# A decoder layer with attention, RWKV-7 and 32 experts: the second norm applied behind the router and row transposes, both moved into the output projection; selection on whole tiles; outputs in pairs

## The chip, the cores and the metric

One core of one Trainium2 chip. The metric is the device time of one execution in microseconds.

## What is computed

One layer for 256 prompt tokens and 8 sample tokens (T = 264), D = 1024, all float32. Attention and RWKV-7 mixing give `m`; then

```
x  = x + gate1(c) * (m @ w_o)
h2 = rms_norm(x, norm2) * (1 + scale2(c)) + shift2(c)
logits = h2 @ w_router + b_router              # 32 experts
top 4 per token, gates = softmax of those 4
y  = sum over chosen experts of gate * (swiglu(h2 @ w1[e] + b1[e]) @ w2[e] + b2[e])
x  = x + gate2(c) * y
```

`c` is one vector for the prompt and one for each sample. Caches and states are outputs too.

## The kernel before

Everything is kept with features on the 128 partitions: `XT` and `HT` are `[128, 8 chunks, 264 tokens]`. Each engine has its own hand-written program in `build`, joined by semaphores; a `group()` on TensorE and its twin on ScalarE hand out four PSUM banks in turn, in the order of `a_order`. `chain(...)` makes VectorE wait for its own last instruction. SyncE (SP) streams all weights in chunks of 2 MB into ring slots 0 to 5 and later two slots (6, 7) in `arena`, each issued when the slot's last user is done.

Ahead of the experts TensorE runs, in line order: modulation 10 and its transpose, modulation 11 (L1174 to 1176, the modulation matmuls at L812, 32 columns each, four beside each other), group-norm sums (L1179), mixers `pa` and `pb` (L1190), the output projection (L1203: eight steps of eight matmuls, banks 4 to 7), eight sums of squares (L1207). VectorE adds the residual (L1655 to 1658); ScalarE squares (L688). Then VectorE computes the norm for each token (L1363 to 1365) and `h2` in two halves (L1374 to 1378), TensorE the router product (L1214), 24 transposes of `h2` to token rows (L1222) which ScalarE copies into `XR` (L698), and transposes of the logits (L1227).

Selection (L1679 to 1738, VectorE) takes the best 8 of 32 per token for three token tiles (128, 128, 8), builds a 0/1 mask `MSK` with one comparison and three accumulating ones per tile (L1685, L1687); TensorE turns the mask into each token's position in its expert by triangular products (L1234, L1238); VectorE makes ranks `POSM` (L1704, L1710) and 64 slots per expert (L1721). A round serves 64 tokens of every expert; here there is one round.

Expert i on TensorE: four chunks of `w1` (L1296), combine of expert i-1 (L1269) which VectorE adds to `YA` (L1749), transposes (L1304), gather of the next expert's rows through `OH` (L1245, copy L714 or L727, transposes L1251, copy L716 or L733), two chunks of `w2` (L1323). Line 369 loads the last two chunks of expert 0 when the projection is done; lines 376 onward load each next chunk when its slot is used. At the end: combine, eight updates of `XT` (L1778), 24 transposes (L1338), six copies on ScalarE (L741), three stores (L393).

```
for c in (4, 2):
    sp.wait_ge(*chunk_used(max(i for i in range(len(stream)) if slots_of[i] == c)))
    sp.dma_start(slot_tile(c, c), expert_chunk(0, c)).then_inc(sem[f"ring{c}"], 16)
```

## Time and profile before

| | us |
|---|---|
| median of 3 runs | 1339.03 (1333.54 to 1339.52) |
| profiled execution | 1338.93 |
| its span | 1337.1 |
| TensorE busy | 1259.7 (94%) |
| VectorE, ScalarE busy | 452.7, 300.6 |
| DMA | 467.03 MB, 349 GB/s mean |

The span runs from the first to the last recorded instruction. Matmul busy time overlaps (matmuls are pipelined), so it doesn't say how near TensorE is to its limit. A float32 matmul is recorded as two instructions, a transpose as one.

### The profile page before, as it was taken

To read this page: it belongs to the slowest core of one execution; us is meant where nothing else is said; L and a number is where in the kernel's file an instruction comes from. 1 tells how busy PE (TensorE), PEld (TensorE's weight loads), DVE (VectorE), ACT (ScalarE), POOL (GpSimd) and SP (SyncE) were. 2 spreads that over 40 slices of the span, in tenths; PEclk is the share of its full clock that TensorE was granted. 3 is DMA by queue.
4 is the path that set the end of the run, shared out by engine and by line. 5 is a ranking of instruction groups with operands and counts; after the bars stand their busy time and mean duration, and the time that the engine had idled before them with its cause. 6 is when DMAs were issued, how large, how long until landed. Compare 5 with 4: busy or idle time off the path is not lost.

```text
span 1337.1 us, 21010 instructions
## 1 busy us (share of the span) xinstructions
PE 1259.7 (94%) x8316; PEld 633.5 (47%) x8316; DVE 452.7 (34%) x1062; ACT 300.6 (22%) x553; POOL 53.8 (4%) x67
## 2 busy tenths in 40 slices
PE   6998997989969999999999999999999999999997
PEld 4787776977833334333333333333333333333333
DVE  2145658335262223322233222233222223322223
ACT  3012441211022112222122121222121122212112
POOL 0000530300000000000000000000000000000000
PEclk9899998999979999999999999999999999999999
DMA  9966351139437999999999999999999999999993
GB/s 368 344 233 246 111 162 59 40 132 376 194 126 308 425 429 428 428 430 428 428 428 429 428 429 428 429 429 428 429 428 428 429 428 428 428 430 427 429 428 134
DMA packets 55606, 467.03 MB, mean 349 GB/s; under 512 B 5141, under 2 KB 7449, under 8 KB 29690
## 3 DMA queue, kind: packets, MB, share of 16 engines
q1 hardware_dynamic: 53354, 461.05, 83.0%
q0 software_dynamic: 1664, 5.20, 1.4%
q8 instruction: 35, 0.57, 0.2%
q10 hardware_dynamic: 544, 0.13, 0.0%
q14 instruction: 9, 0.07, 0.0%
HBM read 463.89 MB, written 5.09 MB: 351 GB/s over the span
## 4 chain that ended last, share of the span: by engine, by line
PE 72%; DMA 20%; DVE 4%; ACT 2%; issue 1%; SPq 0%; DVEq 0%
PE ps L1296 24%; DMA ring<-in_w 18%; PE ps L1323 13%; PE ps L1245 5%; PE ps L843 5%; PE ps L1269 4%; PE ps L833 3%; PE ps L1203 2%; PE ps L1304 2%; DMA ring<-in_w_mod 2%; PE ps L1190 1%; PE ps L1251 1%; PE ps L852 1%; ACT PT L727 1%; PE ps L812 1%
## 5 line engine op out<-in xcount | busy, mean ns | idle before, releaser
L1296 PE MATMUL ps<-ring,PT 128*64 128x512 f32 x1536 | 337.5, 593 | 10.7 <-DMA ring<-in_w 9.9
L1749 DVE TENSOR_TENSOR SQ<-ps,SQ 128x528 f32<-128x528 f32 x132 | 84.1, 699 | 617.9 <-PE ps L1269 617.9
L1296 PEld LDWEIGHTS ps<-ring,PT 128*64 128x64 f32 x1536 | 109.6, 137 | 232.7 <-issue 209.0
L1323 PE MATMUL ps<-ring,PT 128*64 128x512 f32 x768 | 170.1, 596 | 0.0
L722 ACT COPY HT<-ps 128x512 f32<-128x512 f32 x64 | 34.4, 589 | 396.9 <-PE ps L1296 396.9
L1296 PE MATMUL ps<-arena,PT 128*64 128x512 f32 x512 | 113.5, 593 | 3.9 <-DMA arena<-in_w 3.9
L1323 PEld LDWEIGHTS ps<-ring,PT 128*64 128x64 f32 x768 | 53.2, 137 | 99.8 <-issue 99.8
L1245 PE MATMUL ps<-XR,PT 128*64 128x512 f32 x396 | 93.9, 610 | 1.6 <-DVE PT L1721 1.6
L1269 PE MATMUL ps<-PT 64*128 64x264 f32 x528 | 76.3, 408 | 0.8 <-ACT PT L735 0.8
L1296 PEld LDWEIGHTS ps<-arena,PT 128*64 128x64 f32 x512 | 36.5, 137 | 78.2 <-issue 69.1
L843 PE MATMUL ps<-HT,ring 128*128 128x264 f32 x304 | 70.7, 394 | 0.0
L1269 PEld LDWEIGHTS ps<-PT 64*128 64x128 f32 x528 | 45.3, 185 | 44.9 <-issue 27.6
L735 ACT COPY PT<-ps 128x512 f32<-128x512 f32 x32 | 18.8, 586 | 206.1 <-PE ps L1323 206.1
L843 PEld LDWEIGHTS ps<-HT,ring 128*128 128x128 f32 x304 | 58.6, 194 | 10.8 <-issue 0.8
L833 PE MATMUL ps<-HT,ring 128*128 128x264 f32 x208 | 54.3, 414 | 4.9 <-DMA ring<-in_w_in 3.5
L1323 PE MATMUL ps<-arena,PT 128*64 128x512 f32 x256 | 56.7, 596 | 0.0
L1245 PEld LDWEIGHTS ps<-XR,PT 128*64 128x64 f32 x396 | 25.9, 138 | 46.0 <-issue 46.0
L833 PEld LDWEIGHTS ps<-HT,ring 128*128 128x128 f32 x208 | 40.5, 202 | 14.2 <-DMA ring<-in_w_in 3.8
L722 ACT ACT_TABLE_LOAD x32 | 41.1, 1283 | 0.9 <-issue 0.4
L725 ACT ACT_TABLE_LOAD x32 | 41.1, 1283 | 0.6
L1727 DVE TENSOR_SCALAR PT<-cst,PT 128x128 f32<-128x128 f32 (+1 forms) x96 | 27.1, 339 | 28.4 <-DVE PT L1770 25.8
L1304 PE MATMUL ps<-cst,HT 128*128 128x128 f32 x256 | 35.0, 280 | 0.0
(383 smaller groups left out, 1153.9 us busy)
## 6 DMA issues: line engine op xcount, KB each, us to landing
ring<-in_w SPq DMA_DIRECT2D x144, 2048.0 KB, 28.9
arena<-in_w SPq DMA_DIRECT2D x48, 2048.0 KB, 28.8
ring<-in_w_mod SPq DMA_DIRECT2D x12, 2048.0 KB, 12.7
ring<-in_w_in SPq DMA_DIRECT2D x9, 2048.0 KB, 14.9
ring<-in_w_o SPq DMA_DIRECT2D x2, 2048.0 KB, 16.6
ring<-in_w_pa SPq DMA_DIRECT2D x1, 2048.0 KB, 12.8
ring<-in_w_pb SPq DMA_DIRECT2D x1, 2048.0 KB, 9.2
bias_rows<-bias_by_distance POOLq DMA_DIRECT2D x1, 1536.0 KB, 14.0
```

Of the source, the lines that this page charges most:

```text
L722: act.copy(UR[:, h, :].rearrange("p (f r) -> p f r", f=4), ps[:, 2 + h, :].rearrange("p (r f) -> p f r", f=4)).then_inc(sem["ur_evac"], 1)
L725: act.activation(US_, UG, ACT.Sigmoid, scale=1.702).then_inc(sem["us_ready"], 1)
L833: last = mm(ps[:, GATE_BANK[b], 0:T], w[:, k, s * P:s * P + P], HT[:, k, :], start=(k == 0), stop=(k == KD - 1))
L843: last = mm(bank[:, 0:T], w[:, k, s * P:s * P + P], HT[:, k, :], start=(k == 0), stop=(k == KD - 1))
L1203: last = mm(ps[:, 4 + k % 4, 0:T], w[:, i, (k % 4) * P:(k % 4) * P + P], HT[:, i, :], start=(i == 0), stop=(i == KD - 1))
L1245: last = mm(ps[64 * s:64 * s + 64, 0, :], OH[:, n, :], XR[:, n, s * 512:s * 512 + 512], start=(n == 0), stop=(n == 2))
L1269: last = mm(ps[:, bank + s, 0:T], YS[64 * s:64 * s + 64, p * P:p * P + P], GT[64 * s:64 * s + 64, :], start=True, stop=True)
L1296: last = mm(ps[64 * lin:64 * lin + 64, 2 + hh, :], XG[:, k % 4, k // 4, :], slot_tile(slot, c)[:, k % 2, lin * FE + hh * 512:lin * FE + hh ...
L1304: last = tr(ps[:, 2 + hh, f * P:f * P + P], UR[:, hh, f * P:f * P + P], ID)
L1323: last = mm(ps[64 * hh:64 * hh + 64, 4, :], AC[:, f, :], slot_tile(slot, c)[:, f % 4, hh * 512:hh * 512 + 512], start=(f == 0), stop=(f == ...
L1727: v.tensor_scalar(OG[0:nt, n, :], IO2[0:nt, :], POSM[0:nt, n, col], GATE[0:nt, n, col], ALU.is_equal, ALU.mult)
L1749: v.tensor_tensor(YA[:, p::4, :], ps[:, bank:bank + 2, 0:T], YA[:, p::4, :], ALU.add).then_inc(sem["comb_used"], 1)
```

## The change

- The norm is no longer applied before router and transposes. ScalarE and VectorE form `Z = x * norm2 * (1 + scale2)`; router and row transposes work on `Z`, and the per-token factor `1/rms` is applied to the logits and, by ScalarE's scaled copies, to the rows of the two prompt tiles. The shift's part of the logits is computed ahead (`CX`, `CL`), the shift's part of the rows is row 8 of the third tile in `XR` (samples hold their difference to it), which every slot gathers.
- Row transposes of step k-1 and half of the router product stand inside the projection, which uses two banks in place of four. Router matmuls go to four column groups and are summed in a product with `K_S4`. Squares are summed on VectorE into `ACC`, and across partitions with one column.
- Selection runs on whole tiles: one comparison and one reduction for the mask, positions in six products, first gather ahead of gates, ranks of later rounds and `GTE`.
- The slots of the two large tiles are compared in one instruction in every expert; the third tile has nine rows.
- At the end the sum so far is applied before the last combine, whose four pairs go straight to `XT`; copies of the outputs are shared by ScalarE and VectorE.
- The clearing of `YA` on GpSimd waits for the first gather; the router bias is loaded as one row; `MR` moves to `RS`. On VectorE, behind the key norm (L1448), the bias of modulation columns 24 to 32 is added and the sample differences `DSX` are formed.

New and kept lines of the diff (removed lines and unnamed edits are left out; the kernel before stands above):

```diff
+c[:, K_S4:K_S4 + NE] = p % NE == np.arange(NE)
...
+Z, SQ1, MSK4 = SQ, view(PT, 2582, 2, T), view(PT, 3110, 3, 4, NE)
+CX, CL = RS[:, P:P + 136], view(PT, 2318, 2, NE)
+DSX, brr, x1s = view(SSf, 0, KD, 9), SSf[0:1, 72:72 + NE], SSf[:, 104:112]
...
+    pool.wait_ge(sem["h2r_done"], 3)
+    pool.wait_ge(sem["xg_evac"], 1)
     pool.memset(YA[:, :, :], 0.0).then_inc(sem["comb_used"], 1)
...
+    bank = group()
+    act.copy(CX[:, 0:P], bank[:, 0:1].broadcast_to([P, P]))
+    act.copy(CX[:, P:P + NS], bank[:, 1:9]).then_inc(sem["a_evac"], 1)
+    act.wait_ge(sem["st_kv"], 64)
+    for s in range(2):
+        bank = group_bank()
+        act.copy(pairs_apart(XR[0:9, 2, s * 512:s * 512 + 512]), pairs_read(bank[0:9, :])).then_inc(sem["a_evac"], 1)
     mod_rows(11)
...
+    bank = group()
+    act.copy(CL[:, 0, :], bank[:, 0:NE])
+    act.copy(CL[0:NS, 1, :], bank[0:NS, NE:2 * NE]).then_inc(sem["a_evac"], 1)
     for k in range(KD):
+        act.wait_ge(sem["x1_ready"], 2 * k + 1)
+        act.mul(Z[:, k, 0:NP], XT[:, k, 0:NP], A1[:, k, 0:1]).then_inc(sem["zp_ready"], 1)
         act.wait_ge(sem["x1_ready"], 2 * k + 2)
...
+        if k >= 3:
+            act.wait_ge(sem["acc_done"], k - 2)
+        act.activation(SQ1[:, k % 2, :] if k else ACC, XT[:, k, :], ACT.Square).then_inc(sem["sq2_ready"], 1)
     act.wait_ge(sem["ms_ready"], 2)
...
+    act.activation(st[:, 70:73], st[:, 70:73], ACT.Sqrt).then_inc(sem["sqrt_done"], 1)
+    act.wait_ge(sem["rs_ready"], 1)
+    act.wait_ge(sem["st_s"], 32)
+    for n in range(2):
+        act.wait_ge(sem["h2r_done"], n + 1)
+        for s in range(2):
+            act.mul(pairs_apart(XR[:, n, s * 512:s * 512 + 512]), pairs_read(ps[:, 2 * n + s, :]),
+                    st[:, 70 + n:71 + n]).then_inc(sem["h2r_evac"], 1)
+    act.wait_ge(sem["top_ready"], 1)
+    act.activation(RNK[:, :, :], LG[:, :, :], ACT.Exp).then_inc(sem["top_exp"], 1)
...
+    pe.wait_ge(sem["ld_r"], 32)
+    bank = group()
+    for k in range(KD):
+        g = k % 4
+        mm(bank[32 * g:32 * g + NE, 0:9], wr[:, k, :], modT[:, 24 + k, :], start=(k < 4), stop=(k >= 5))
+    mm(bank[0:NE, 0:9], brr, ONE[0:1, 0:9], start=False, stop=True).then_inc(sem["a_done"], 1)
+    for s in range(2):
+        bank = group()
+        for k in range(4):
+            last = tr(bank[0:9, k * P:k * P + P], DSX[:, 4 * s + k, :], ID)
+        last.then_inc(sem["a_done"], 1)
     modulation(11)
...
+    bank = group()
+    pe.wait_ge(sem["a_evac"], a_end("cl"))
+    mm(bank[:, 0:NE], CX[:, 0:P], cst[:, K_S4:K_S4 + NE], start=True, stop=True)
+    mm(bank[0:NS, NE:2 * NE], CX[:, P:P + NS], cst[:, K_S4:K_S4 + NE], start=True, stop=True).then_inc(sem["a_done"], 1)
+    def rows(k, tiles):
+        for n in tiles:
+            t0, nt = TILES[n]
+            bank = 2 * n + k // 4 if n < 2 else 6 - k // 4
+            last = tr(ps[0:nt, bank, (k % 4) * P:(k % 4) * P + P], Z[:, k, t0:t0 + nt], ID)
+        return last
+    def logits(ks):
+        for k in ks:
+            last = mm(ps[32 * (k % 4):32 * (k % 4) + NE, 7, 0:T], wr[:, k, :], Z[:, k, :], start=(k < 4), stop=(k >= 4))
+        return last
     for k in range(KD):
         w = weights("wo", k // 4)
...
+        if k >= 2:
+            pe.wait_ge(sem["x1_ready"], 2 * k - 2)
         for i in range(KD):
...
+            last = mm(ps[:, 4 + k % 2, 0:T], w[:, i, (k % 4) * P:(k % 4) * P + P], HT[:, i, :], start=(i == 0), stop=(i == KD - 1))
         last.then_inc(sem["wo_done"], 1)
...
+        if k == 1:
+            pe.wait_ge(sem["a_evac"], a_end("cm"))
+        if k:
+            pe.wait_ge(sem["zp_ready"], k)
+            pe.wait_ge(sem["zs_ready"], k)
+            rows(k - 1, range(3 if k <= 4 else 2))
+        if k == 4:
+            logits(range(4))
+    pe.wait_ge(sem["zp_ready"], KD)
+    pe.wait_ge(sem["zs_ready"], KD)
+    logits(range(4, KD)).then_inc(sem["lg_done"], 1)
+    pe.wait_ge(sem["acc_done"], KD - 2)
+    pe.wait_ge(sem["sq2_ready"], KD)
+    for n, (t0, nt) in enumerate(TILES):
+        mm(ps[0:nt, 4, 96 + n:97 + n], ACC[:, t0:t0 + nt], ONE[:, 0:1], start=True, stop=False)
+        last = mm(ps[0:nt, 4, 96 + n:97 + n], SQ1[:, 1, t0:t0 + nt], ONE[:, 0:1], start=False, stop=True)
     last.then_inc(sem["ss_done"], 1)
...
+    pe.wait_ge(sem["lgt_ready"], 1)
+    for n, (t0, nt) in enumerate(TILES):
+        last = mm(ps[0:nt, 7, 320 + n * NE:320 + n * NE + NE], LGT[:, t0:t0 + nt], cst[:, K_S4:K_S4 + NE], start=True, stop=True)
+    last.then_inc(sem["lg_done"], 1)
+    for n in range(2):
+        rows(KD - 1, [n]).then_inc(sem["h2r_done"], 1)
+    for k in range(4, KD):
+        last = rows(k, [2])
+    last.then_inc(sem["h2r_done"], 1)
     pe.wait_ge(sem["msk_ready"], 1)
...
+    mm(ps[:, 4, 160:256], ONE, MSK[:, 0:1, :].broadcast_to([P, 3, NE]), start=True, stop=False)
+    mm(ps[:, 4, 160:192], cst[:, K_US:K_US + P], MSK[:, 1, :], start=False, stop=False)
+    mm(ps[:, 4, 192:256], ONE, MSK[:, 1:2, :].broadcast_to([P, 2, NE]), start=False, stop=False)
+    mm(ps[:, 4, 192:224], cst[0:NS, K_US:K_US + P], MSK[0:NS, 2, :], start=False, stop=False)
+    mm(ps[:, 4, 224:256], ONE[0:NS, :], MSK[0:NS, 2, :], start=False, stop=True)
+    mm(ps[:, 4, 128:160], cst[:, K_US:K_US + P], MSK[:, 0, :], start=True, stop=True).then_inc(sem["pos_done"], 1)
...
+        for n, rows_in in enumerate((P, P, NS + 1)):
             for s in range(2):
...
+                last = mm(ps[64 * s:64 * s + 64, 0, :], OH[0:rows_in, n, :], XR[0:rows_in, n, s * 512:s * 512 + 512],
+                          start=(n == 0), stop=(n == 2))
         last.then_inc(sem["xr_done"], 1)
...
+    pe.wait_ge(sem["h2r_evac"], 4)
+    pe.wait_ge(sem["h2s_ready"], 1)
     pe.wait_ge(sem["oh_ready"], 1)
     gather()
+    pe.wait_ge(sem["xr_evac"], 1)
+    gather_transposed()
     pe.wait_ge(sem["gte_ready"], 1)
     scatter_transposed(GTE)
...
     pe.wait_ge(sem["rounds_ready"], 1)
...
+    pe.wait_ge(sem["ys_evac"], rounds * NE + 1)
+    pe.wait_ge(sem["gt_evac"], rounds * NE + 1)
+    pe.wait_ge(sem["comb_used"], rounds * (NE * 4) + 1)
+    def outputs(p, tiles):
+        for n in tiles:
+            t0, nt = TILES[n]
+            for s in range(2):
+                last = tr(ps[0:nt, 2 * n + s if n < 2 else 6 + s, p * P:p * P + P], XT[:, 4 * s + p, t0:t0 + nt], ID)
+        return last
+    for p in range(4):
+        if p >= 2:
+            pe.wait_ge(sem["x2_ready"], p - 1)
+        for s in range(2):
+            last = mm(ps[:, 4 + 2 * (1 - p % 2) + s, 0:T], YS[64 * s:64 * s + 64, p * P:p * P + P], GT[64 * s:64 * s + 64, :],
+                      start=True, stop=True)
+        last.then_inc(sem["comb_done"], 1)
+        if p >= 2:
+            outputs(p - 2, range(2))
+    pe.wait_ge(sem["x2_ready"], 3)
+    outputs(2, range(2))
+    for p in range(3):
+        outputs(p, [2])
+    pe.wait_ge(sem["x2_ready"], 4)
+    outputs(3, [0]).then_inc(sem["fin_done"], 1)
+    outputs(3, [1]).then_inc(sem["fin_done"], 1)
+    outputs(3, [2]).then_inc(sem["fin_done"], 1)
...
     dve.wait_ge(sem["a_evac"], a_end("modT11"))
...
+    for lo, hi in ((16, 24), (32, 48)):
+        out, bias = add_bias(lo, hi)
+        chain(v.tensor_tensor(out, out, bias, ALU.add))
     chain(v.tensor_scalar(modT[:, 16:24, :], modT[:, 16:24, :], 0.5, None, ALU.mult))
+    chain(v.scalar_tensor_tensor(out=A1[:, :, :], in0=modT[:, 32:40, :], scalar=1.0,
+                                 in1=PC[:, PCOL["norm2"]:PCOL["norm2"] + KD].unsqueeze(2).broadcast_to([P, KD, 9]),
+                                 op0=ALU.add, op1=ALU.mult))
+    v.memset(st[:, 70:73], 1.0)
+    v.memset(LG, 0.0)
+    v.memset(POSM, 0.0)
+    chain(v.memset(GTE, 0.0))
     for k in range(KD):
         dve.wait_ge(sem["wo_done"], k + 1)
...
+        src = ps[:, 4 + k % 2, :]
+        chain(v.tensor_tensor(x1s, src[:, NP:T], modT[:, 16 + k, 1:9], ALU.mult))
         v.scalar_tensor_tensor(out=XT[:, k, 0:NP], in0=src[:, 0:NP], scalar=modT[:, 16 + k, 0:1],
                                in1=XT[:, k, 0:NP], op0=ALU.mult, op1=ALU.add).then_inc(sem["x1_ready"], 1)
...
+        done(v.tensor_tensor(XT[:, k, NP:T], XT[:, k, NP:T], x1s, ALU.add), "x1_ready", 2 * k + 2)
+        v.tensor_tensor(Z[:, k, NP:T], XT[:, k, NP:T], A1[:, k, 1:9], ALU.mult).then_inc(sem["zs_ready"], 1)
+        if 1 <= k < KD - 1:
+            dve.wait_ge(sem["sq2_ready"], k + 1)
+            done(v.tensor_tensor(ACC, ACC, SQ1[:, k % 2, :], ALU.add), "acc_done", k)
     IE = cst[:, K_IE:K_IE + NE]
...
     dve.wait_ge(sem["lg_done"], 1)
...
+    v.tensor_copy(LGT, ps[:, 7, 0:T]).then_inc(sem["lgt_ready"], 1)
+    dve.wait_ge(sem["ss_done"], 2)
+    v.tensor_scalar(st[:, 70:72], ps[:, 4, 96:98], 1.0 / D, 1e-5, ALU.mult, ALU.add)
+    v.tensor_scalar(st[0:NS, 72:73], ps[0:NS, 4, 98:99], 1.0 / D, 1e-5, ALU.mult, ALU.add).then_inc(sem["ms_ready"], 1)
+    dve.wait_ge(sem["sqrt_done"], 2)
+    done(v.reciprocal(st[:, 70:73], st[:, 70:73]), "rs_ready", 1)
+    dve.wait_ge(sem["a_evac"], a_end("cm"))
     dve.wait_ge(sem["lg_done"], 2)
...
+    tiles(lambda n, nt: v.scalar_tensor_tensor(out=LG[0:nt, n, :], in0=ps[0:nt, 7, 320 + n * NE:320 + n * NE + NE], scalar=st[0:nt, 70 + n:71 + n],
+                                               in1=CL[0:nt, n // 2, :], op0=ALU.mult, op1=ALU.add))
+    tiles(lambda n, nt: v.max(mx8[:, n, :], LG[:, n, :]))
+    tiles(lambda n, nt: v.max_index(ix8[:, n, :], mx8[:, n, :], LG[:, n, :]))
+    chain(v.tensor_copy(ixf[:, :, :], ix8[:, :, :]))
+    chain(v.tensor_tensor(MSK4, IE.unsqueeze(1).unsqueeze(1).broadcast_to([P, 3, 4, NE]),
+                          ixf[:, :, 0:4].unsqueeze(3).broadcast_to([P, 3, 4, NE]), ALU.is_equal))
+    done(v.tensor_reduce(MSK[:, :, :], MSK4.rearrange("p n j e -> p n e j"), AX.X, ALU.add), "msk_ready", 1)
+    v.tensor_tensor(LG[:, :, :], LG[:, :, :], mx8[:, :, 0:1].broadcast_to([P, 3, NE]), ALU.subtract).then_inc(sem["top_ready"], 1)
+    dve.wait_ge(sem["h2r_done"], 3)
+    for s in range(2):
+        for b in range(2):
+            lo = b * 2 * P
+            rows_of_x = XR[0:NS, 2, s * 512 + lo:s * 512 + lo + 2 * P].rearrange("t (j p) -> t j p", j=2)
+            last = v.scalar_tensor_tensor(out=rows_of_x, in0=ps[0:NS, 6 - s, lo:lo + 2 * P].rearrange("t (p j) -> t j p", j=2),
+                                          scalar=st[0:NS, 72:73], in1=rows_of_x, op0=ALU.mult, op1=ALU.add)
+    last.then_inc(sem["h2s_ready"], 1)
     dve.wait_ge(sem["pos_done"], 1)
...
+    tiles(lambda n, nt: v.scalar_tensor_tensor(out=POSM[0:nt, n, 0:NE], in0=ps[0:nt, 4, 128 + n * NE:160 + n * NE], scalar=1.0,
+                                               in1=MSK[0:nt, n, :], op0=ALU.add, op1=ALU.mult))
...
     def gather_slots(col):
...
+        v.tensor_tensor(OH[:, 0:2, :], IO.unsqueeze(1).broadcast_to([P, 2, C]), POSM[:, 0:2, col].broadcast_to([P, 2, C]), ALU.is_equal)
+        return v.tensor_scalar(OH[0:NS + 1, 2, :], IO[0:NS + 1, :], cst[0:NS + 1, K_BB:K_BB + 1], POSM[0:NS + 1, 2, col],
+                               ALU.mult, ALU.is_equal)
...
     gather_slots(slice(0, 1)).then_inc(sem["oh_ready"], 1)
...
+    chain(v.tensor_reduce(st[:, 80:81], ps[:, 4, 224:256], AX.X, ALU.max))
...
+    dve.wait_ge(sem["top_exp"], 1)
+    chain(v.tensor_tensor(RNK[:, :, :], RNK[:, :, :], MSK[:, :, :], ALU.mult))
+    chain(v.tensor_reduce(st[:, 73:76], RNK[:, :, :], AX.X, ALU.add))
+    chain(v.reciprocal(st[:, 73:76], st[:, 73:76]))
+    chain(v.tensor_tensor(RNK[:, :, :], RNK[:, :, :], st[:, 73:76].unsqueeze(2).broadcast_to([P, 3, NE]), ALU.mult))
+    done(v.tensor_copy(GTE.rearrange("p n (s e) -> p n s e", s=2)[:, :, :, 0:NE], RNK[:, :, :].unsqueeze(2).broadcast_to([P, 3, 2, NE])), "gte_ready", 1)
+    chain(v.tensor_copy(GATE[:, :, 0:MAXR * NE].rearrange("p n (r e) -> p n r e", e=NE),
+                        RNK[:, :, :].unsqueeze(2).broadcast_to([P, 3, MAXR, NE])))
+    for q in range(1, MAXR):
+        tiles(lambda n, nt: v.tensor_scalar(POSM[0:nt, n, q * NE:q * NE + NE], POSM[0:nt, n, 0:NE], -1.0 * q * C, None, ALU.add))
...
+    dve.wait_ge(sem["comb_used"], rounds * (NE * 4) + 1)
     chain.base, chain.count = rounds * (NE * LINKS) + links_before, 0
     chain(v.tensor_tensor(YA[:, :, NP:T], YA[:, :, NP:T], modT[:, 40:48, 1:9], ALU.mult))
...
+    v.tensor_tensor(XT[:, :, NP:T], XT[:, :, NP:T], YA[:, :, NP:T], ALU.add)
     for k in range(KD):
         last = v.scalar_tensor_tensor(out=XT[:, k, 0:NP], in0=YA[:, k, 0:NP], scalar=modT[:, 40 + k, 0:1],
                                       in1=XT[:, k, 0:NP], op0=ALU.mult, op1=ALU.add)
+    chain(last)
+    for p in range(4):
+        bank = 4 + 2 * (1 - p % 2)
+        dve.wait_ge(sem["comb_done"], rounds * (NE * 4) + p + 1)
+        chain(v.tensor_tensor(YA[:, p::4, NP:T], ps[:, bank:bank + 2, NP:T], modT[:, 40 + p:48:4, 1:9], ALU.mult))
+        v.tensor_tensor(XT[:, p::4, NP:T], XT[:, p::4, NP:T], YA[:, p::4, NP:T], ALU.add)
+        for s in range(2):
+            k = 4 * s + p
+            last = v.scalar_tensor_tensor(out=XT[:, k, 0:NP], in0=ps[:, bank + s, 0:NP], scalar=modT[:, 40 + k, 0:1],
+                                          in1=XT[:, k, 0:NP], op0=ALU.mult, op1=ALU.add)
         last.then_inc(sem["x2_ready"], 1)
+    for n, (_, nt) in enumerate(TILES):
+        dve.wait_ge(sem["fin_done"], n + 1)
+        v.tensor_copy(fin[0:nt, n, 512:D], ps[0:nt, 2 * n + 1 if n < 2 else 7, :]).then_inc(sem["fin_half"], 1)
```

## Rows read from the trace of the kernel before

**Rows 1.** Windows: us busy (instructions) per engine, granted clock, DMA share, GB/s

```profile
395.00:400.00 5.00, 3.92 (x12) 1.26 (x12) 3.20 (x25) 0.00 (x0) 0.00 (x0) 0.55 0.00 0
...
405.00:410.00 5.00, 5.00 (x26) 1.72 (x24) 0.00 (x0) 0.00 (x0) 0.00 (x0) 1.00 0.41 108
...
600.00:900.00 300.00, 297.59 (x1486) 112.71 (x1484) 84.81 (x226) 68.79 (x105) 0.00 (x0) 1.00 1.01 429
```

**Rows 2.** Chain of waits, expert loop: start us, us, what

```profile
403.43 13.95 PE ps L1296 x64
...
488.12 13.73 PE ps L1296 x64
...
516.27 13.73 PE ps L1296 x64
...
1245.01 3.65 PE ps L1296 x16
...
1303.74 3.65 PE ps L1296 x16
```

**Rows 3.** Line 369, the two loads behind the output projection

```profile
DMA to landing us min/median/max: 7.6/9.8/12.1
```

**Rows 4.** Timeline ahead of the projection: start us, us, engine, operation, [idle before <-releaser]

```profile
126.33 1.04 PE L892 MATMUL ps<-cst,PT 128*9 128x128 f32 x8
...
286.67 0.47 PE L1168 MATMUL ps<-cst,arena 128*128 128x32 f32 x2 [2.54 <-issue]
...
303.86 1.95 PE L812 MATMUL ps<-ring,cT 128*32 128x128 f32 x64
...
309.16 6.75 DVE L1631 RECIPROCAL SQ<-SQ 128x1056 f32<-128x1056 f32 x1 [11.93 <-ACT SQ L683]
...
320.46 3.83 PE L1190 MATMUL ps<-PT,ring 128*128 128x264 f32 x16 [0.20 <-DVE HT L1627]
```

**Rows 5.** Chain of waits, output projection to gather

```profile
339.53 28.75 PE ps L1203 x128
...
368.28 3.57 PE ps L1207 x16
...
392.89 1.57 PE ps L1238 x6
...
396.07 4.46 PE ps L1245 x12
```

**Rows 6.** Timeline, projection to first expert, and a gather in the loop

```profile
386.41 1.09 PE L1222 MATMUL ps<-cst,HT 128*128 128x128 f32 x8
...
389.01 1.76 DVE L1687 SCALAR_TENSOR_TENSOR arena<-cst,ixf,arena 128x32 f32<-128x32 f32 x9
...
401.37 0.59 ACT L714 COPY PT<-ps 128x512 f32<-128x512 f32 x1
...
420.58 2.80 PE L1245 MATMUL ps<-XR,PT 128*64 128x512 f32 x12
```

**Rows 7.** Groups of instructions, 339 to 404 us: busy us, mean ns of one

```profile
L1656 DVE SCALAR_TENSOR_TENSOR XT<-ps,modT,XT 128x256 f32<-128x256 f32 x8 | 3.9, 484 | 0.3
...
L688 ACT ACTIVATE SQ<-XT 128x264 f32<-128x264 f32 x8 | 3.4, 423 | 57.1 <-DVE XT L1658 57.1
...
L1374 DVE TENSOR_TENSOR HT<-XT,RS 128x1056 f32<-128x1056 f32 x2 | 2.5, 1254 | 0.0
...
L1655 DVE TENSOR_TENSOR A<-ps,modT 128x8 f32<-128x8 f32 x8 | 1.3, 167 | 23.0 <-PE ps L1203 23.0
```

**Rows 8.** Windows with short pauses of TensorE, columns as in rows 1

```profile
226.00:230.00 4.00, 3.17 (x42) 2.06 (x36) 3.80 (x4) 0.39 (x1) 1.27 (x1) 1.00 0.34 79
...
285.00:288.00 3.00, 1.33 (x5) 1.16 (x6) 1.65 (x5) 0.00 (x0) 0.00 (x0) 0.80 0.78 232
```

**Rows 9.** Timeline of the tail

```profile
1322.58 2.31 PE L1269 MATMUL ps<-PT 64*128 64x264 f32 x16 [0.76 <-ACT PT L735]
...
1333.27 0.72 SPq L393 DMA_DIRECT2D out_y_sample<-ring  x1
```

204 lines of the change are left out of this document (40 added, 164 removed).

## The prediction

> **What bounds the kernel now.** I read the busy shares by window first, then the chain of waits in order of time, then the timelines of three places. In the long middle both TensorE and the DMA engines look full [rows 1]. The chain tells them apart. In the first half of the expert loop one expert follows the next on TensorE every 516.27 - 488.12 = 28.15 us. Late in the loop the chain runs through weight loads, and two experts take 1303.74 - 1245.01 = 58.73 us, so 29.37 us each [rows 2]. A chunk of 2 MB (2.097 million bytes) at 429 GB/s takes 4.9 us [rows 1], six of them 29.3; the loop begins limited by TensorE, with eight chunks in hand, loses 1.2 us of that lead on each expert, and ends limited by the DMA stream. So a faster or slower expert body would change nothing as long as it stays under 29.4 us.
>
> What matters is when the stream restarts. In the window from 395 to 400 us the DMA share is 0.00: every slot is full, and the next chunk waits for expert 0 to use its first one. It restarts between 405 and 410 us (share 0.41), some 3.7 us after the first expert matmul at 403.43 [rows 1, 2], and is full from there on. About 182 chunks of 4.9 us follow before the last one on which the chain waits. A microsecond by which the first expert starts earlier is therefore a microsecond off the end, as long as it does not start before expert 0's last two chunks have landed, up to 12.1 us after the output projection [rows 3]. The other place that counts is the tail behind the last load.
>
> The change adds work on TensorE ahead of the output projection, lengthens the projection, and shortens what lies between it and the first expert.
>
> **Ahead of the projection.** Between the transpose of modulation 10 and modulation 11 TensorE gets nine small packed matmuls (18 instructions) and eight transposes of nine columns. The packed modulation runs 64 instructions in 1.95 us, so 18 take 0.55; eight such transposes took 1.04 [rows 4]. That is 1.6 us. Behind it come modulation 11, the group-norm sums, the square root and the 6.75 us reciprocal on VectorE, which the last mixer chunks wait for (TensorE stands 0.20 us until a VectorE result at 320.46) [rows 4]. So I count all 1.6 on the path; the bounds are 0, if the delay is absorbed, and 2.5, if ScalarE's four new copies stand in front of its row copy. The two VectorE subtractions far ahead, behind the key norm, cost nothing: VectorE then waits for the decay, and no queue is behind them. The wait of ScalarE for the k and v stores costs nothing either; they were issued over 100 us before. The constant's last product is four instructions straight in front of the projection; two with 128-column weights took 0.47 [rows 4], so 0.7, between 0.4 and 0.9. The new preamble on VectorE (bias in two parts, A1, four memsets) is about 2.1 us and hides behind the first 3.6 us of the projection; without that cover it would be paid in full.
>
> **In the projection.** It takes 28.75 us for 128 instructions, 0.225 each [rows 5]. Eighteen transposes go between its steps, one pair of them behind its last. Eight back to back took 1.09 [rows 6], so 0.136 each: 2.2 us ahead of the end. Four router matmuls go in beside each other on four column groups: as two instructions of 264 columns 0.45, as eight 1.8; packed, like the modulation, I take 0.45. With two banks in place of four, step k waits for the evacuation of k-2, a whole step of 3.6 us old, and the transposes for a copy that is ready about 1.25 us after its step (VectorE 0.17 and 0.48, ScalarE 0.42) [rows 7]. VectorE's work per step grows to some 1.9 us. No new wait bites. The projection ends at 368.28 + 1.6 + 0.7 + 2.2 + 0.45 = 373.2.
>
> **From there to the first expert.** Before: 403.43 - 368.28 = 35.15 us. It held eight sums of squares (3.57) [rows 5], the norm and modulation on VectorE, router product, 24 transposes, and a selection in small steps. Now, in order:
> - last residual and scaled copy 1.25, second half of the router product 0.45
> - sums of squares: eight wide instructions by 0.223 and four narrow by 0.1, 2.2
> - mean, square root and reciprocal of three columns 1.05; beside them the transposing product of the logits
> - scaling, max and index at the spacing of the old small steps, 1.3; cast 0.2; one comparison of 384 elements and one reduction. A 256-element operation took 0.484 and a 1056-element one 1.254 [rows 7], so 0.6 each. In all 2.7
> - positions: twelve instructions with 128-column weights. Six took 1.57 [rows 5]: 3.1. The four row fix-ups of the sample tile (about 2.0 on VectorE) lie beside them; if positions took less than 2, they would be late next
> - ranks 0.4, slots 0.5, handing over 0.1: 1.0
> - gather 4.0. It took 4.46 here and 2.80 inside the loop [rows 5, 6]; I take nearly the first, because the granted clock was 0.55 from 395 to 400 [rows 1], mostly the lower level of 1.2 GHz, and TensorE will again stand some 2 us before the positions. After a pause of 2.54 us up to 286.67 the granted clock was 0.80 in the window around its end [rows 4, 8]
> - copy, four transposes, copy: 403.43 - 401.37 [rows 2, 6], and 0.15: 2.2. The gate's copy no longer stands in front.
>
> The sum is 17.95 us. The first expert then starts at 391.2, 12.2 earlier. The gates, further ranks and the round count run on VectorE until about then, and the loop's first need of them is 14 us later. The zeroing of YA moves from under the old norm to under the first expert, 1.9 us on GpSimd with 12 in hand.
>
> A rule speaks against the size of one term. The nine accumulations of the old mask took 1.76 us, 0.195 each for 32 elements [rows 6]; with the three comparisons before them they are 2.3, and two operations of 0.6 give back 1.1. The Trainium skill (VectorE: DVE Perf Modes, the errata section) has 58 cycles at 0.96 GHz plus one per element for an operation in SBUF; by it the twelve would be 1.1 us, the two 0.9, and merging would give back 0.2. This trace doesn't agree with its price of a small operation; by its price of the two large ones the end would come 0.3 sooner, at 1323.8. I go by the rows.
>
> **Inside an expert.** Three comparisons become two and the last gather tile has nine rows; TensorE streams the same columns. Under the DMA limit this is worth nothing.
>
> **The tail.** Before, the last combine starts at 1322.58; four additions, two small steps and eight updates follow, TensorE transposes behind them, and the last of six copies lets the third store go at 1333.27, 3.8 us before the end [rows 9]. Now all but the last expert is added in while the last products run. Each of four pairs takes 0.17 + 0.16 + two of 0.48 overlapping, 1.25, from 1323.1: the last at 1328.2. Two transposes for each large tile, one pair of copies on two engines each 0.6, the last store at 1330.7: 2.6 us sooner, between 1.5 and 3.5.
>
> **The sum** is made against the profiled execution, 1338.93 us (span 1337.1 and 1.8 around it), 0.1 under the median of 1339.03: 1338.93 - 12.2 - 2.6 = 1324.1.
>
> **Rivals.**
> A. Clock kept and the insertion hidden: new TensorE pauses are 1 to 2 us, and from 226 to 230, with TensorE busy 3.17 of 4 us in short bursts, it stayed at 2.4 GHz [rows 8]. Then positions 0.5, the gather 1.2 and upstream up to 1.6 less: 1320.8. Against it, the window after 284 [rows 8]. Chance 0.20.
> B. Dearer chain: VectorE's broadcast comparison and transposed reduction, which the trace doesn't show, at twice my price (1.2), router matmuls not packed (2.7 for both halves), fix-ups late (1.0), a tail worth only 1.5: 1330.1. Chance 0.10.
> C. The stream doesn't restart with the first expert, and only the tail is gained: 1336.3. For it, the DMA share stays at 1.01 through the loop; against it, the idle 25 us in front [rows 1]. Chance 0.05.
> D. Slower: the per-expert chain passes the DMA period. The slot comparisons for the next expert feed TensorE's gather; the two-input form with broadcasts would have to hold VectorE until TensorE waits in every expert. From 29.4 us on each added microsecond costs 31, so it must add 1.2 before it decides; at 2.0 the end is 0.8 x 31 - 14.8 = 10 us later, 1349. Against it: VectorE is busy 84.81 of 300 us in the loop [rows 1]. Chance 0.03.
> E. It doesn't do what it says, or router values change the number of rounds: no change or far slower. 0.02.
>
> **Numbers.** The forecast itself has 0.60 and runs from 1321.5 to 1327.5. Taking in A and half of B, the range is 1317.5 to 1330.5. A measurement of this kernel can tell about 0.5%, 6.7 us, from no change; below 1332.3 is faster. That is the forecast, A and B: 0.90. Within 0.5% are C and half of E: 0.06. Slower are D and the other half: 0.04.
>
> **What would show it.** The first expert matmul near 391; the projection's end near 373, modulation 11 1.6 later; selection ready about 7.7 after the projection; DMA restarting at about 395; the same 29.4 us between late experts; the last store issued 2.6 sooner after the last combine. It is wrong if the projection shows gaps of its own, if ScalarE is the releaser ahead of modulation 11 or the square root, or if experts take over 29.4.

## The result, and the profile after

The changed kernel takes 1322.76 us (median, 1321.98 to 1327.27) against 1339.15 of the kernel before: ratio 0.9894, 95% interval 0.986 to 0.9928. The forecast was 1324.1. It was right in sign and size, but what follows from modulation 10 on became only 11.7 to 12.3 us shorter, where 14.8 were forecast; the rest of the 16 us lies ahead of modulation 10, where no gain was forecast. Single executions of the kernel before at 1483 to 1485 us, with a granted clock of 0.84, are left out of every comparison.

The page of the changed kernel begins so (busy us, share of the span, instructions):

```profile
span 1321.2 us, 21010 instructions
PE 1259.3 (95%) x8339; PEld 626.5 (47%) x8339; DVE 453.8 (34%) x1034; ACT 300.1 (23%) x554; POOL 52.9 (4%) x66
```

The chain of waits of the changed kernel, from modulation 10 to the last expert (start us, us, what):

```profile
297.06 1.93 PE ps L834 x64
301.09 1.93 PE ps L834 x64
306.32 6.76 DVE SQ L1687
...
871.18 13.73 PE ps L1347 x64
...
899.48 6.89 PE ps L1347 x32
906.53 31.58 DMA ring<-in_w
...
1231.94 3.65 PE ps L1347 x16
...
1290.68 3.65 PE ps L1347 x16
```

The last chunk is waited for at 1290.68 instead of 1303.74 [rows 2], 13.1 sooner. The reader can also see where the loop changes hands: until 906 one expert follows the next on TensorE, behind that the chain runs through the loads, 1290.68 - 1231.94 = 58.74 for two experts, as before [rows 2].

The stretch between the output projection and the first expert, in the timeline of the changed kernel (start us, us, engine, line, operation, idle before and its releaser):

```profile
369.87 0.66 PE L1246 MATMUL ps<-SQ,arena 128*32 128x264 f32 x8 [1.17 <-ACT SQ L715]
370.46 0.38 PE L1270 MATMUL ps<-cst,arena 128*128 128x1 f32 x2
...
371.72 0.16 DVE L1732 TENSOR_SCALAR st<-ps 128x2 f32<-128x2 f32 x1 [0.69 <-PE ps L1271]
...
372.54 0.56 DVE L1745 SCALAR_TENSOR_TENSOR arena<-ps,st,PT 128x32 f32<-128x32 f32 x3 [0.15 <-PE ps L1275]
...
374.38 0.56 DVE L1750 TENSOR_TENSOR PT<-cst,ixf 128x384 f32<-128x384 f32 x1
374.97 0.80 DVE L1752 TENSOR_REDUCE arena<-PT 128x96 f32<-128x384 f32 x1
...
375.83 0.74 PE L1284 MATMUL ps<-arena,cst 128*128 128x96 f32 x2 [2.62 <-DVE arena L1752]
...
378.96 0.37 DVE L1764 SCALAR_TENSOR_TENSOR PT<-ps,arena 128x32 f32<-128x32 f32 x3 [1.33 <-PE ps L1289]
...
380.02 5.58 PE L1295 MATMUL ps<-XR,PT 128*64 128x512 f32 x12 [1.10 <-DVE PT L1772]
...
388.16 15.62 PE L1347 MATMUL ps<-ring,PT 128*64 128x512 f32 x64
```

The last line is from the timeline of TensorE alone. The projection's last step ends at 368.50, so this chain is 19.66 us long; before it was 35.15. And its tail, behind the last product:

```profile
1309.67 1.16 PE L1397 MATMUL ps<-PT 64*128 64x264 f32 x8 [0.76 <-ACT PT L759]
...
1317.55 0.50 SPq L406 DMA_DIRECT2D out_y_sample<-ring  x1
```

From the last combine to the end of the span: 1321.2 - 1309.67 = 11.53, before 1337.1 - 1322.58 = 14.52 [rows 9].

Where the 15.49 us between projection and first expert were won can be read off the two timelines, with two lines of the kernel before:

```profile
386.52 0.37 DVE L1679 COPY arena<-ps 128x32 f32<-128x32 f32 x3 [0.43 <-PE ps L1227]
...
388.45 0.52 DVE L1685 TENSOR_SCALAR arena<-cst,ixf 128x32 f32<-128x32 f32 x3
```

From the projection's end to VectorE's first reading of the logits for the selection (386.52 before, 372.54 now) it is 18.24 and 4.04 us: 14.2 of the 15.49, against 4.4 us more work ahead of that point. The selection up to the positions took 4.37 (386.52 to 390.89) and takes 3.29, positions to gather 5.18 and 4.19, and the gather with what follows it 7.36 and 8.14, which is 0.8 dearer.

**The head.** Not all of the gain lies where the change is. In the chains of waits modulation 10 starts at 301.27 before and at 297.06 after, and ahead of it the two kernels do the same work but for a few small steps of VectorE (a bias, a subtraction, a copy). PE timelines of the early part, first the kernel before, then the changed one:

```profile
28.77 3.64 PE L798 MATMUL ps<-ring,cT 128*32 128x128 f32 x64 [2.79 <-DMA ring<-in_w_mod]
36.02 16.97 PE L852 MATMUL ps<-HT,ring 128*128 128x264 f32 x64 [1.79 <-DVE HT L1399]
```

```profile
28.98 2.59 PE L820 MATMUL ps<-ring,cT 128*32 128x128 f32 x83 [1.45 <-issue]
34.70 14.48 PE L874 MATMUL ps<-HT,ring 128*128 128x264 f32 x64 [1.79 <-DVE HT L1451]
```

From 18 to 36 us the granted clock is 0.76 before and 1.00 after. So I measure everything from the start of modulation 10 to the end of the span: 1035.83 before, 1024.14 after. From there on the change is worth 11.7; some four of the 16 us are ahead of it.

### The profile page after: what moved, and what is told of

It reads as the page before. It is cut to its first block, busy times and chain, and to the rows that moved or that the text cites. A ratio compares the mean times of both kernels' runs of the same rounds, so it can differ in the third digit from the quotient of the medians.

```text
span 1321.2 us, 21010 instructions
## 1 busy us (share of the span) xinstructions
PE 1259.3 (95%) x8339; PEld 626.5 (47%) x8339; DVE 453.8 (34%) x1034; ACT 300.1 (23%) x554; POOL 52.9 (4%) x66
## 4 chain that ended last, share of the span: by engine, by line
PE 73%; DMA 18%; DVE 5%; ACT 2%; issue 1%; SPq 0%; DVEq 0%
PE ps L1347 24%; DMA ring<-in_w 18%; PE ps L1374 13%; PE ps L1295 6%; PE ps L865 5%; PE ps L1320 4%; PE ps L1254 2%; PE ps L855 2%; PE ps L1355 2%; PE ps L1222 1%; PE ps L1302 1%; ACT PT L751 1%; PE ps L874 1%; PE ps L834 1%; PE ps L1118 1%
## 5 line engine op out<-in xcount | busy, mean ns | idle before, releaser
L1295 PE MATMUL ps<-XR,PT 128*64 128x512 f32 (+1 forms) x396 | 99.7, 622 | 1.1 <-DVE PT L1772 1.1
L1295 PEld LDWEIGHTS ps<-XR,PT 128*64 128x64 f32 (+1 forms) x396 | 22.8, 136 | 53.5 <-issue 53.5
```

Source lines behind the costliest of these rows:

```text
L1295: last = mm(ps[64 * s:64 * s + 64, 0, :], OH[0:rows_in, n, :], XR[0:rows_in, n, s * 512:s * 512 + 512], start=(n == 0), stop=(n == 2))
```

## The experiments

**The head again: is it the program or the run?** The changed kernel unchanged, and the kernel before unchanged.

> The changed kernel once more. In the two profiles at hand it is 15.9 us shorter in span, but 3.8 us of that are there before 53 us, where the two programs are the same: the clock rose at about 20 us in the one and at about 14 us in the other, which then lost it in the wait for weights. Theory A (the front is a matter of the clock's phase in an execution, not of the change): times of both kernels fall in two groups 4 to 5 us apart, and group against group the change is worth 11 to 12.5 us, ratio 0.991. Rival B (the change moves the front): all runs of the changed kernel have the short front, and it stays 15 to 16 us faster, ratio 0.988.

Measured 1323.05 (1322.17 to 1323.68), ratio 0.9891, interval 0.9872 to 0.991. Modulation 10 at 297.75, from there 1023.55. The ratio lies between the two theories. (The rise of the clock "at about 14" and "at about 20 us" is read from durations: the same pair of matmuls takes 1.25 us before and 0.71 behind it. The granted clock of these windows reads 1.00 in both profiles.)

> The kernel before, once more, for a second profile of it. From the start of modulation 11's predecessor (modulation 10 on TensorE) to the end of the span the kernel before took 1035.9 us, the changed kernel 1024.1 and 1023.6 in two profiles; ahead of it the same instructions took 301.2 against 297.1 and 297.8. Theory A (that head is a matter of the clock's phase in each execution): here modulation 10 starts anywhere from 296 to 302, and what follows takes 1035.9 again. Rival B (the change shortens the head): it starts at 301 again.

Measured 1335.47 us in one execution. In its PE timeline the fourth modulation chunk is fast, and the first projection is 0.8 us shorter and begins two microseconds sooner:

```profile
28.31 1.96 PE L798 MATMUL ps<-ring,cT 128*32 128x128 f32 x64 [2.31 <-DMA ring<-in_w_mod]
...
34.14 16.19 PE L852 MATMUL ps<-HT,ring 128*128 128x264 f32 x64 [2.52 <-DMA ring<-in_w_in]
```

Modulation 10 starts at 297.85, where the changed kernel has it, and from there it takes 1035.85, as in the first profile of before. So the same program runs with either head. At equal heads the two kernels stand at 1335.47 and 1323.05: 12.4 us, and 12.3 from modulation 10 on.

Two things about the head stay open. The first is where it comes from: the clock of the first 36 us is a part of it only. In the run a_full (below) that clock is 0.76 as in the first profile of before, and modulation 10 still starts at 297.74; in a_loop1 and a_loop3 it is 0.97 and 0.96, and modulation 10 starts at 300.52 and 300.34. A second place is a piece of 16 projection matmuls behind a pause of 2.53 us shortly ahead of modulation 10: it takes 5.16 us in the changed kernel and 6.68 in a_loop3, where the granted clock behind the pause stays at 0.50 for longer. The second is whether the change has a part in how often a kernel gets the short head. All executions of the kernel before, over four sessions, have a median of 1337.5 (37 of them, 1333.4 to 1340.0, 11 below 1335.6); the nine of the changed kernel have 1323.0, and eight of them lie between 1321.9 and 1323.7. That is 14.5 us between medians, two more than at equal heads. Nothing here shows whether this is chance or the change.

**Can the head be held?** The kernel before with idle matmuls in the waits of its first 36 us.

```
                 slot = slots_of[STREAM_AT["modA", q]]
+                filler((0, 1, 1, 6)[q], 7)
...
+            filler(1, 7)
             pe.wait_ge(sem["mod_a_evac"], 1)
...
             last.then_inc(sem["setup_t"], 1)
+            filler(3, 7)
```

> The kernel before, with matmuls on spare PSUM columns put where TensorE waits for the first weights and the first norm (before the third and fourth modulation chunk, before the transposes and before the first projection). Theory A: the granted clock stays at 1.00 from 25 to 45 us, the first projection (line 852) takes 14.4 us instead of 17.0, and the kernel ends about 4 us sooner than the kernel before in its slower group (about 1334 to 1335), with little scatter. Rival B: no change of the end, because the weights of later projections arrive no sooner.

Measured 1337.69 (1333.88 to 1342.79), ratio 1.0003, interval 0.9987 to 1.0018: nothing. Its timeline tells why (lines of this kernel):

```profile
32.72 1.95 PE L804 MATMUL ps<-ring,cT 128*32 128x128 f32 x64
...
37.83 14.48 PE L860 MATMUL ps<-HT,ring 128*128 128x264 f32 x64 [0.49 <-DVE HT L1407]
```

The clock was held, 14.48 instead of 16.97. But the fillers were more than the waits: the fourth modulation chunk came at 32.72 instead of 28.77, and the projection 1.8 later. Behind the projection this profile is 0.7 us ahead of the first one of before and 2.0 behind the second: what the clock gave, the filling took. It then lost another 2.1 us up to modulation 10, which starts at 302.69; with one profile of twelve executions that part isn't explained.

**Chain: what does the clock cost?** In the changed kernel the granted clock falls in the short pauses behind the projection and stays down through dense work, the gather included. Windows of the changed kernel (length, busy us of PE, PEld, DVE, ACT, POOL, granted clock, DMA share, GB/s):

```profile
370.00:375.00 5.00, 3.21 (x32) 2.28 (x28) 3.11 (x19) 2.56 (x6) 0.00 (x0) 0.95 0.87 364
375.00:380.00 5.00, 3.09 (x12) 2.79 (x13) 3.57 (x12) 1.77 (x3) 0.00 (x0) 0.50 0.99 423
380.00:385.00 5.00, 4.98 (x12) 1.13 (x12) 4.00 (x24) 0.00 (x0) 0.00 (x0) 0.50 0.01 3
385.00:390.00 5.00, 4.18 (x15) 1.95 (x15) 1.75 (x2) 2.53 (x4) 1.83 (x1) 0.50 0.00 0
390.00:395.00 5.00, 5.00 (x22) 1.55 (x20) 0.85 (x5) 0.30 (x1) 0.03 (x1) 0.84 0.27 49
```

Eleven idle matmuls of 256 columns were spread there, into columns of banks 4 and 7 that nothing reads any more (VectorE raises `lg_read` when it has read the logits out of bank 7):

```
+            for _ in range(2):
+                mm(ps[:, 4, 256:512], XT[:, 0, 0:P], XT[:, 1, 0:256], start=True, stop=True)
             pe.wait_ge(sem["zp_ready"], KD)
...
+            pe.wait_ge(sem["lg_read"], 1)
+            filler(5)
             pe.wait_ge(sem["msk_ready"], 1)
...
+            filler(2)
             pe.wait_ge(sem["h2r_evac"], 4)
...
             gather()
+            filler(1)
...
             scatter_transposed(GTE)
+            filler(1)
...
+            dve.sem_inc(sem["lg_read"], 1)
```

> The changed kernel with matmuls of 256 columns on spare PSUM columns where TensorE waits: two behind the projection, five before the positions (behind VectorE's reading of the logits), two before the first gather, one behind it, one behind the gate's transposes. Theory A (all from the positions to the first expert's second chunk runs at the lower clock because of the pauses): positions 2.4 instead of 3.1 us, gather 2.9 instead of 5.0 to 5.6, first expert's w1 part 13.95 instead of 15.6; the load stream restarts about 5 us sooner and the end comes 4 to 6 us sooner. Rival C (the gather is slow because of its nine-row tile or late row copies): the same durations, and the fillers cost up to 1 us.

Measured 1319.16 (1317.36 to 1319.66), ratio 0.9866, interval 0.9847 to 0.9884. Its windows and its timeline, first expert included:

```profile
375.00:380.00 5.00, 4.52 (x26) 3.26 (x26) 4.67 (x18) 2.35 (x4) 0.00 (x0) 1.00 0.99 426
380.00:385.00 5.00, 4.94 (x25) 1.97 (x23) 3.54 (x21) 1.45 (x3) 0.53 (x1) 1.00 0.13 56
...
390.00:395.00 5.00, 5.00 (x27) 1.59 (x24) 0.00 (x0) 0.00 (x0) 0.00 (x0) 1.00 0.91 374
```

```profile
376.54 0.46 PE L1293 MATMUL ps<-arena,cst 128*128 128x96 f32 x2 [0.32 <-DVE arena L1765]
...
379.42 2.94 PE L1304 MATMUL ps<-XR,PT 128*64 128x512 f32 x12 [0.15 <-DVE PT L1785]
...
384.63 13.95 PE L1359 MATMUL ps<-ring,PT 128*64 128x512 f32 x64
```

The clock stays at 1.00. The gather takes 2.94 instead of 5.58 (4.96 in the second profile), positions to gather 2.9 instead of 4.2, the first expert's first part 13.95 instead of 15.62, and it starts at 384.63. The load stream restarts at 388.33 instead of 393.53. From modulation 10 to the end 1017.95: 5.6 to 6.2 less than in the two profiles of the changed kernel. That is the price of the lower clock in this stretch, and it reaches the end. Rival C, a gather slowed by its nine-row tile or by late row copies, is out: the same gather runs in 2.94.

**Transposes behind the logits.** All 24 row transposes go behind the router product, so that the projection carries none.

```
-                if k:
+                if k == 4:
                     pe.wait_ge(sem["zp_ready"], k)
                     pe.wait_ge(sem["zs_ready"], k)
-                    rows(k - 1, range(3 if k <= 4 else 2))
...
+            for n in range(3):
+                for k in range(KD):
+                    last = rows(k, [n])
+                last.then_inc(sem["h2r_done"], 1)
```

> The changed kernel with all row transposes behind the logits instead of inside the output projection (the router product stays inside). The projection loses 18 transposes, so it ends 2.2 us sooner; the 24 transposes, 3.2 us, lie where TensorE waits for the selection (2.6 us idle there, and 0.9 us of transposes already). Theory A: the first expert starts 1.5 to 2.2 us sooner or more, since TensorE pauses less and the clock may stay up, up to 5 us sooner at the end. Rival D (putting the transposes into the projection was what made the chain short): the rows are copied too late, the gather waits for ScalarE, and the end is the same or up to 1 us later.

Measured 1319.29 (1313.26 to 1323.01), ratio 0.9861, interval 0.9834 to 0.9888; from modulation 10 1020.24, 3.3 less than the second profile of the changed kernel. (This count, here and below, rests on one profile for each run; the two of the changed kernel differ by 0.6 in it, the two of the kernel before by less than 0.1.) So one part of the change, the transposes inside the projection, was a loss in this kernel. The 24 transposes take TensorE's pause under the selection. Its PE timeline:

```profile
369.06 4.51 PE L1240 MATMUL ps<-cst,SQ 128*128 128x128 f32 x24
373.40 0.36 PE L1281 MATMUL ps<-arena,cst 128*128 128x96 f32 x2
...
376.23 4.59 PE L1292 MATMUL ps<-XR,PT 128*64 128x512 f32 x12 [1.15 <-DVE PT L1769]
```

24 transposes in 4.51 are 0.188 each; inside the projection a group of three is recorded with 0.49, and the next projection matmul starts 0.33 behind it. The projection itself is 1.76 shorter (29.53 instead of 31.29). The granted clock was 0.68 from 370 to 375 although TensorE was busy all of the 5.00 us; with fillers around the same 24 they took 2.84, below. So this run gained from the shorter projection and still paid for the clock.

**The insertion ahead.** The shift constants and the nine-column transposes go to an earlier pause, behind the carry and ahead of the sample's output product.

```
             pe.wait_ge(sem["carry_evac"], 5)
+            bank = ps[:, 0, :]
+            for k in range(KD):
+                g = k % 4
+                mm(bank[32 * g:32 * g + NE, 0:9], wr[:, k, :], modT[:, 24 + k, :], start=(k < 4), stop=(k >= 5))
...
+            for s in range(2):
+                bank = group()
+                for k in range(4):
+                    last = tr(bank[0:9, k * P:k * P + P], DSX[:, 4 * s + k, :], ID)
...
             pe.wait_ge(sem["ot_ready"], 1)
...
             modulation_transposed(10)
...
-            for s in range(2):
-                bank = group()
-                for k in range(4):
-                    last = tr(bank[0:9, k * P:k * P + P], DSX[:, 4 * s + k, :], ID)
-                last.then_inc(sem["a_done"], 1)
             modulation(11)
```

> The changed kernel with the shift's constant product and the eight sample-difference transposes moved from between modulation 10 and 11 to TensorE's pause of 2.5 us before the sample output product (their ScalarE copies with them). Theory A (they stand on the path where they are, at 1.4 us, and the pause lets the clock fall): modulation 11 follows modulation 10's transpose at once; the end comes 1.4 us sooner, and up to 1.4 more if the projection piece behind the pause (16 instructions, 5.0 us) runs at the full clock, 3.6. Rival D (slack between modulation 11 and the mixers absorbs them): no change, within 0.5 us.

Measured 1320.39 (1318.83 to 1322.15), ratio 0.9871, interval 0.9847 to 0.9894. PE timeline:

```profile
285.39 3.81 PE L866 MATMUL ps<-HT,ring 128*128 128x264 f32 x16
...
298.03 1.96 PE L835 MATMUL ps<-ring,cT 128*32 128x128 f32 x64
...
300.69 1.95 PE L835 MATMUL ps<-ring,cT 128*32 128x128 f32 x64
```

Modulation 11 follows 2.66 behind modulation 10, as in the kernel before, where the changed kernel has 4.03. From modulation 10 1021.8, 1.7 less. The sixteen matmuls behind the pause take 3.81 instead of 5.16 in the changed kernel's timeline, at a granted clock of 1.00 from 284 to 286 instead of 0.56. That is a second gain of the work in the pause, and one that lies outside that count.

**What is a microsecond in the loop worth?** The prediction said nothing, up to a period of 29.4. Three more matmuls per expert in one run, one in the other (range(1)):

```
                 pe.wait_ge(sem["comb_used"], 4 * i + 4)
+                for _ in range(3):
+                    mm(ps[:, 5, 0:256], HT[:, 5, 0:P], HT[:, 6, 0:256], start=True, stop=True)
                 gather_transposed()
```

> The changed kernel with three more matmuls of 256 columns in every expert on TensorE, 0.43 us each, so 1.3 us. Counted over all 32 experts the loop takes 28.77 us each, with 28.30 of TensorE work and 29.4 of loads less the eight chunks in hand. Theory A (the lead makes the loads' bound 28.77 on the mean): TensorE's 29.59 decides, 32 x 0.82 = 26 us later. Rival E (what I said in the prediction, that nothing counts under 29.4): 0.2 x 31, some 6 us later. Rival F (TensorE bounds every expert already): 32 x 1.29 = 41 us later.

Measured 1353.5 (1352.37 to 1354.58), ratio 1.0119, interval 1.0098 to 1.014; modulation 10 at 300.34, from there 1052.2, 28.6 more than the changed kernel. Its chain runs on TensorE to the end:

```profile
1280.87 13.73 PE ps L1347 x64
1310.51 13.73 PE ps L1347 x64
```

> The changed kernel with one more matmul of 256 columns per expert, between combining and the gather's transposes. Three of them made the TensorE-bound period 29.65 instead of 28.30, so one makes it 28.75, against a mean of 28.77 per expert at which the loads arrive. Theory A (loads and TensorE are nearly level, and only what passes 28.77 counts): the time stays at 1323 to 1325. Theory F (TensorE's own work sets the loop): 32 x 0.45 = 14.4 more, 1337.5. The prediction's own statement expects no change here too; it failed at three.

Measured 1326.05 (1323.38 to 1328.05), ratio 0.9916, interval 0.9899 to 0.9933; modulation 10 at 300.52, from there 1024.5, 0.9 more. Its chain:

```profile
1255.19 13.73 PE ps L1347 x64
1283.96 13.73 PE ps L1347 x64
```

The period is 28.77 and never waits for a load. In the changed kernel the loop's mean is the same (1309.67 - 388.16 over 32 experts, 28.80), though its TensorE-bound experts take 28.30: they only use up the chunks in hand, and wait later. So 28.8 is the point at which loads and TensorE are level over 32 experts. With 29.64 each expert is (29.64 - 28.77) dearer, 32 times 27.8 us, and 28.6 was measured. The free slack is 0.47 us per expert, not 1.1. No run has a period between 28.8 and 29.4, where the two readings differ most plainly; what tells them apart is the cost at 29.64.

**Nine rows or 128.** In the loop a gather takes 2.90 in the changed kernel's chain and took 2.75. Its third tile got 128 rows again, the rest zeros.

```
-                for n, rows_in in enumerate((P, P, NS + 1)):
+                for n, rows_in in enumerate((P, P, P)):
...
+            chain(act.mul(XR[:, 2, :], XT[:, 0:4, 0:256], 0.0))
...
-                return v.tensor_scalar(OH[0:NS + 1, 2, :], IO[0:NS + 1, :], cst[0:NS + 1, K_BB:K_BB + 1], POSM[0:NS + 1, 2, col],
+                return v.tensor_scalar(OH[:, 2, :], IO, cst[:, K_BB:K_BB + 1], POSM[:, 2, col],
```

> The changed kernel with a gather of three tiles of 128 rows again: ScalarE fills the third tile of the rows with zeros before modulation 11's rows (about 1 us of ScalarE), and the gather's third tile and its slots have 128 rows instead of nine. Theory A (the third tile of nine rows makes the gather slower, 2.90 instead of 2.75 us, and the loads hide it): the gather in the loop takes 2.75, the period of TensorE-bound experts 28.15, the time stays within 1 us of 1323.0. Theory B (the loop is bound by TensorE for most experts): the time falls by up to 32 x 0.15 = 4.8, to 1318. Theory C (the nine rows are not the cause): the gather in the loop stays at 2.90.

Measured 1320.98 (1318.52 to 1323.26), ratio 0.988, interval 0.9862 to 0.9899. In its timeline and that of the changed kernel, the same gather:

```profile
1266.31 2.80 PE L1296 MATMUL ps<-XR,PT 128*64 128x512 f32 x12
```

```profile
1268.16 2.94 PE L1295 MATMUL ps<-XR,PT 128*64 128x512 f32 x12
```

The nine rows cost 0.14 per expert, and the loads hide it: from the first expert to the last wait for a chunk this run takes 900.5 us, and the run with fillers, whose gather has nine rows and whose first part takes 13.95 too, 900.4. From modulation 10 it is 1021.5, 2.0 less; 1.7 of it is the first expert's first part, 13.95 instead of 15.65. In both profiles the granted clock is back at 1.00 from 386 to 388; in the second profile of the changed kernel it falls to 0.50 again from 390 to 392, here it stays. Whether the larger tile has a part in that, one profile doesn't show. In the loop itself the gather's size did nothing.

**The old tail.** The changed kernel with the last combine, addition and outputs of before: the pre-addition and the pairs are gone, six output groups, all copied by ScalarE.

```
+            combine(rounds * NE)
+            for i in range(6):
...
+            accumulate(rounds * NE)
+            dve.wait_ge(sem["comb_used"], rounds * (NE * 4) + 5)
```

> The changed kernel with the tail of the kernel before: the last combine into the sum of the experts, the whole final addition behind it, six output groups of four transposes, all copied by ScalarE. Theory A (the outputs in pairs were worth what the two tails differ by): from the end of the products to the end of the span 12.2 becomes 15.1, the time 1325.9, ratio to the kernel before 0.9915. Theory B (the tail is set by the last store and its landing, so half of it comes back): 1324.4. The stretch ahead of the tail is as in the changed kernel.

Measured 1326.5 (1325.15 to 1327.94), ratio 0.9921, interval 0.9907 to 0.9935. PE timeline:

```profile
1312.05 2.31 PE L1321 MATMUL ps<-PT 64*128 64x264 f32 x16 [0.76 <-ACT PT L758]
1317.71 4.51 PE L1390 MATMUL ps<-cst,XT 128*128 128x128 f32 x24 [3.36 <-DVE XT L1819]
```

From the last combine to the end 1326.1 - 1312.05 = 14.05, against 11.53: the new tail is worth 2.5. It takes away the 3.36 us in which TensorE waited for VectorE. Against the second profile of the changed kernel another 1.4 us from modulation 10 on lie ahead of the last chunk, outside the tail.

**All three together.** The insertion ahead, all transposes behind the logits, and eight idle matmuls (2, 2, 2, 1, 1).

> The changed kernel with three edits that each ran alone before: the shift constants and sample differences moved ahead of the sample output product, all 24 row transposes behind the logits, and eight idle matmuls spread over the selection and the gather so that TensorE doesn't rest. From the start of modulation 10 to the end the changed kernel needed 1023.6 us, and 1.7 less with the first edit, 3.3 less with the second, 5.6 less with the third. Theory A (the three gains come from different stretches): the second gives only the 2.5 of the 18 transposes inside the projection here, since the rest of its 3.3 was clock, so 1023.6 - 1.7 - 2.5 - 5.6 = 1013.8, and with modulation 10 at 297.7 and 1.7 around the span some 1313. Theory B (the 24 transposes behind the logits now end after the selection mask is ready and hold it up): 1315 to 1317. Theory C (the load stream doesn't start again before S + 5.4 whatever the first expert does): 1318 as with the idle matmuls alone.

Measured 1314.02 (1311.13 to 1316.61), ratio 0.9829, interval 0.981 to 0.9848: faster than both kernels. Timeline and windows:

```profile
368.80 2.84 PE L1247 MATMUL ps<-cst,SQ 128*128 128x128 f32 x24
...
380.53 13.95 PE L1358 MATMUL ps<-ring,PT 128*64 128x512 f32 x64
```

```profile
375.00:380.00 5.00, 4.79 (x23) 1.93 (x22) 4.27 (x26) 0.95 (x2) 0.00 (x0) 1.00 0.30 128
```

The first expert starts 83.9 behind modulation 10 (87.0 with the fillers alone, 90.7 in the changed kernel), 3.1 less, of which 2.4 reach the end: 1015.5 from modulation 10 instead of 1017.95. I had counted on 1013.8. The missing 1.7 can be read off: the insertion gave 1.37 where 1.7 was counted, the shorter projection 1.76 (29.53 instead of 31.30) where 2.5 was counted, and 0.8 is lost between the first expert and the last chunk, 0.4 of it in a wait of 1.25 instead of 0.83 us for that chunk. From the projection's end to the first expert nothing changed, 15.56 and 15.58: the 24 transposes behind the logits held nothing up.

## Why the prediction was right, and where it was not

**Ahead of the projection.** 1.6 for the insertion was 1.37, all on the path, since the reciprocal follows it 1:1; 0.7 for the constant's last product was 0.57. Projection with transposes and router product: 2.65 expected, 2.49 measured (28.75 to 31.24). No gap of its own. Its end came at 368.50 and not 373.2: 4.2 of that is the head, 0.3 the smaller terms.

**From there to the first expert,** 17.95 expected, 19.66 measured:

| term | expected | measured |
|---|---|---|
| last residual, scaled copy, router half | 1.7 | 1.96 |
| sums of squares | 2.2 | 1.16 |
| mean, square root, reciprocal | 1.05 | 0.92 |
| selection | 2.7 | 3.29 |
| positions | 3.1 | 3.13 |
| ranks and slots | 1.0 | 1.06 |
| gather | 4.0 | 5.58 |
| copy, transposes, copy | 2.2 | 2.56 |

The step that failed is "I take nearly the first" for the gather. It took its price from a gather of before that had run in a window of clock 0.55 [rows 1, 5] and gone over to the higher level on its way; here it ran wholly at 1.2 GHz (in the second profile it took 4.96, its end at the higher level). The sums of squares were priced at the width of a projection matmul, though their moving operand is one column: 0.1 each, not 0.223. In the selection the comparison cost 0.56, as taken, the transposed reduction 0.80 instead of 0.6, and the small steps ahead of them 1.84 instead of 1.5. What merging gave back can be read from the two timelines: the mask took 2.32 us before (388.45 to 390.77) and takes 1.39 (374.38 to 375.77), so 0.93, near the 1.1 that went into the sum and far from the 0.2 of the rule that spoke against it. Of the small steps that are left, the three scalings out of PSUM took 0.56, 0.19 each, the price that I took from the rows. But the twelve independent rank steps of 32 elements in SBUF (line 1798) took 1.47, 0.12 each, beside the 0.195 of the old mask. By the cycle table of the Trainium skill (VectorE: DVE Perf Modes, the errata section) an estimate for these twelve is 0.08 to 0.09 each; this trace stands nearer to it there than for the mask. The same section says that this row comes out too low for a single operation, whose fixed term it gives as about 150 cycles; the estimate from that is 0.19, which agrees with the 0.195 of the mask's accumulations, each of which needs the one before it.

**Carried 1:1 to the end** was the largest miss. The first expert started 15.27 sooner, the last chunk was waited for 13.06 sooner. The prediction let the load stream restart 3.7 us behind the first expert matmul, as before; at 1.2 GHz the first part took 15.62 instead of 13.95, the stream restarted at 393.53, 5.4 behind it, and 1.7 of the gain was gone. The rest is within 0.5. Rival A had the right mechanism, the clock, but was taken as the fortunate case: it needed the pauses to be harmless, and they weren't. The run with fillers is what the clock part of A would have been, and it was worth 5.6 to 6.2 us where A had 1.7 for positions and gather: A too left out the first expert and the restart of the stream.

**The tail**: 2.6 expected. Between the profiles the last store is issued 2.8 sooner behind the last combine and the span ends 3.0 sooner behind it; putting the old tail back costs 2.5.

**The loop**: "a faster or slower expert body would change nothing as long as it stays under 29.4" fails. 29.4 is the load period behind a spent lead; over the whole loop the limit is 28.8, and an expert of 29.64 cost all that it was above. It didn't hurt the forecast, since the changed body took 28.30.

**The sum.** From modulation 10 on the change gave 11.7 between the first profiles and 12.3 between the second ones, where 14.8 was forecast. Against the profile that the forecast was made from, 1338.93, that alone is 1326.6 to 1327.2 (an estimate), still inside the forecast's own range, 1321.5 to 1327.5, but at its edge. That the median fell within 1.4 us of 1324.1 is luck: the sum was made against a profile with a long head, the changed kernel was measured with a short one, and the two errors stood against each other.

## To carry to other kernels

Price a gap not by the work in it alone, but by the clock at which the next dense work starts: here eleven idle matmuls, in pauses of one to three microseconds, gave back half as much as the whole restructuring. They pay only where they are shorter than the wait that they fill. Ahead of a stream with chunks in hand, the slack of the loop is the mean over all its iterations, not the distance to the late period. And a difference between two profiles is first cut at the point where the change begins; what lies ahead of it is counted by itself, and is no effect of the change until something shows that it is.

## What the runs showed of the chip that I hadn't expected

- TensorE stayed at 1.2 GHz from 375 to 390 through a gather in which it was busy 4.98 of 5.00 us, and rose only within the first expert. Over the runs without fillers the same 64 matmuls took 15.54 to 15.65 us, and once 13.95.
- Two profiles of the same program, the kernel before, differ by 3.4 us at modulation 10; 2.6 of that is there by the end of the first projection, where the granted clock from 18 to 36 us was 0.76 in the one and 0.95 in the other.
- A gather tile of nine rows is slower than one of 128: 2.94 against 2.80 us for the twelve matmuls, four of which belong to that tile.
- 24 transposes back to back took 4.51 us while the clock fell, and 2.84 while it was held.
